# Adding the squares of three norms up to one tile, with the ones product two contraction tiles later

## The reference

```python
def rmsnorm(x, g):
    xf = x.astype(jnp.float32)
    y = xf * lax.rsqrt(jnp.mean(xf * xf, axis=-1, keepdims=True) + EPS)
    return (y * g.astype(jnp.float32)).astype(x.dtype)

def swiglu(x, w_gate, w_up, w_down):
    return (jax.nn.silu(x @ w_gate) * (x @ w_up)) @ w_down

h = h + 0.5 * swiglu(rmsnorm_2(h, ffn1_norm), ffn1_w_gate, ffn1_w_up, ffn1_w_down)
# mixer, the same norm ahead of it; then
h = h + 0.5 * swiglu(rmsnorm_2(h, ffn2_norm), ffn2_w_gate, ffn2_w_up, ffn2_w_down)
```

## Time and profile before

| | |
|---|---|
| median of 3 runs | 1122.43 us (1122.40 to 1123.10) |
| the profiled execution, its own time | 1122.59 us |
| its span in the trace | 1120.8 us |
| granted TensorE clock, mean | 0.998 of full speed |
| TensorE matmuls busy | 1111.9 us (99%), 8968 |
| VectorE, ScalarE, GpSimd busy | 722.6, 664.2, 731.6 us |

### The profile page before, as it was taken

One profiled execution on the slowest core, in us unless ns is written; L12 is line 12 of the kernel. 1 busy time (PEld: TensorE's weight loads), 2 busy tenths in 40 slices (PEclk: granted clock), 3 DMA queues, 4 the chain that ended last, 5 costly groups with the idle time before them and its releaser, 6 DMA issues.

```text
span 1120.8 us, 22358 instructions
## 1 busy us (share of the span) xinstructions
PE 1111.9 (99%) x8968; PEld 1063.0 (95%) x8968; DVE 722.6 (64%) x1275; ACT 664.2 (59%) x1098; POOL 731.6 (65%) x575
## 2 busy tenths in 40 slices
PE   9999999999999999999999999999999999999997
PEld 7888999999988899899999999999899999999997
DVE  5886655577589675375848655556769567655554
ACT  7676754575567577356647544446566547544444
POOL 6787697668488868865865655445865774544442
PEclk9999999999999999999999999999999999999999
DMA  9563354556555534545566766664644655666651
GB/s 335 172 194 119 129 177 150 177 161 216 159 170 188 161 127 151 176 152 170 189 209 207 223 198 193 195 196 144 215 149 134 206 190 169 220 194 190 189 188 38
DMA packets 63895, 199.49 MB, mean 178 GB/s; under 512 B 6992, under 2 KB 17968, under 8 KB 63792
## 3 DMA queue, kind: packets, MB, share of 16 engines
q1 hardware_dynamic: 61920, 194.99, 53.9%
q10 hardware_dynamic: 1872, 3.08, 0.8%
HBM read 196.21 MB, written 1.84 MB: 177 GB/s over the span
## 4 chain that ended last, share of the span: by engine, by line
PE 96%; ACT 2%; DMA 1%; DVE 0%; issue 0%; POOLq 0%; SPq 0%; ACTq 0%
PE ps L1739 51%; PE ps L1837 19%; PE ps L1815 14%; PE ps L1996 2%; PE ps L1788 1%; PE ps L2173 1%; ACT ring L481 1%; PE ps L2093 1%; DMA x<-in_x 1%; PE ps L2070 1%; PE ps L2031 1%; ACT xs L498 0%; PE ps L1970 0%; PE ps L2057 0%; PE ps L2073 0%; PE ps L2094 0%
## 5 line engine op out<-in xcount | busy, mean ns | idle before, releaser
L367 POOL TENSOR_TENSOR ring<-raw,ring 128x512 fp32r<-128x512 f32 x514 | 699.0, 1366 | 364.2 <-ACT ring L481 343.2
L1739 PE MATMUL ps<-xs,ring 128*128 128x256 f32 x5040 | 597.7, 278 | 0.4 <-DVE mq L1049 0.3
L1739 PEld LDWEIGHTS ps<-xs,ring 128*128 128x128 f32 x5040 | 582.9, 188 | 3.6 <-issue 1.3
L481 ACT ACTIVATE ring<-raw 128x1024 fp32r<-128x1024 f32 x364 | 383.2, 1057 | 215.3 <-PE ps L1739 119.3
L1837 PE MATMUL ps<-ys,ring 128*128 128x256 f32 x1920 | 224.4, 276 | 0.0
L1837 PEld LDWEIGHTS ps<-ys,ring 128*128 128x128 f32 x1920 | 220.7, 188 | 0.0
L1011 DVE TENSOR_TENSOR ring<-raw,ring 128x1024 fp32r<-128x1024 f32 x107 | 144.9, 1355 | 69.3 <-ACT ring L481 68.9
L1815 PE MATMUL ps<-ring,xs 128*128 128x512 f32 x672 | 164.9, 397 | 0.0
L1815 PEld LDWEIGHTS ps<-ring,xs 128*128 128x128 f32 x672 | 123.6, 188 | 26.8 <-issue 1.3
L1329 DVE SCALAR_TENSOR_TENSOR ca<-ps,par,ca 128x253 f32<-128x253 f32 (+2 forms) x96 | 46.0, 479 | 34.4 <-ACT ca L564 33.0
L1483 DVE SCALAR_TENSOR_TENSOR ca<-ps,rms 128x256 f32<-128x256 f32 x44 | 18.6, 423 | 48.7 <-PE ps L1739 48.7
(11 more groups left out here) (291 smaller groups left out, 1027.2 us busy)
## 6 DMA issues: line engine op xcount, KB each, us to landing
raw<-in_w SPq DMA_DIRECT2D x364, 512.0 KB, 3.6
y<-bias_rows SPq DMA_DIRECT2D x6, 256.0 KB, 4.3
out_y<-y SPq DMA_DIRECT2D x4, 256.0 KB, 2.4
const<-in_const SPq DMA_DIRECT2D x1, 896.0 KB, 12.3
bias_rows<-lg ACTq DMA_DIRECT2D x1, 768.0 KB, 8.4
x<-in_x ACTq DMA_DIRECT2D x1, 512.0 KB, 4.5
x<-in_x SPq DMA_DIRECT2D x1, 512.0 KB, 6.9
dec<-in_wT ACTq DMA_DIRECT2D x1, 512.0 KB, 3.7
```

The lines of the kernel that those rows point to most:

```text
L367: last = pool.tensor_tensor(ring[:, g % RING, 1, part], raw[:, g % RAW, part], ring[:, g % RING, 0, part].bitcast(F32), ALU.subtract)
L481: act.activation(ring[:, g % RING, 0, :], raw[:, g % RAW, :], ACT.Copy).then_inc(S["hi"], 1)
L1739: last = mm(ps[bank][:, half * T:(half + 1) * T], ring[:, slot % RING, wp, (at + k) * P:(at + k + 1) * P], rhs(k, xp), start=(first and i ...
```

## The change

At the sites n = 2, 3 and 4 (FOLDED is 2) VectorE adds the two halves of the 128x512 tile once more, to 128x256, and signals `sq_sum` after that. TensorE then runs one ones product instead of two, and runs it after six contraction tiles (18 matmuls) of the third slot instead of four. Sites 0 and 1 stay as they are. (FINAL, 5, is the last norm, which has code of its own.)

```diff
@@ -135,6 +135,7 @@
 N_UPDATES = 4
 FINAL = LAYERS + 3
+FOLDED = LAYERS
 FINAL_AT = (LAYERS + 1) * (KT // 2)
@@ -1027,8 +1028,10 @@
                     dve.wait_ge(S["sq"], n * 4 + b + 1)
                     ins = tt(ps[3][:, :] if b < 3 else sqs[:, 0:512], ps[3][:, :], sqs[:, b * 512:(b + 1) * 512],
                              ALU.add)
-                    if b < 3:
+                    if b < 3 or n >= FOLDED:
                         step(ins)
+                if n >= FOLDED:
+                    ins = tt(sqs[:, 0:T], sqs[:, 0:T], sqs[:, T:2 * T], ALU.add)
                 ins.then_inc(S["sq_sum"], 1)
@@ -1722,8 +1725,9 @@
                 pe.wait_ge(S["sq_sum"], n + 1)
-                for c in range(2):
-                    last = mm(ps[4][:, 0:T], ones, sqs[:, c * T:(c + 1) * T], start=(c == 0), stop=(c == 1))
+                parts = 1 if n >= FOLDED else 2
+                for c in range(parts):
+                    last = mm(ps[4][:, 0:T], ones, sqs[:, c * T:(c + 1) * T], start=(c == 0), stop=(c == parts - 1))
                 last.then_inc(S["ssq"], 1)
@@ -1745,9 +1749,10 @@
             def around_squares(bank, slot, n):
 
-                tile_product(bank, 0, slot, xs_part, range(KT // 2), final=False)
+                ahead = 6 if n >= FOLDED else 4
+                tile_product(bank, 0, slot, xs_part, range(ahead), final=False)
                 sum_squares(n)
-                tile_product(bank, 0, slot, xs_part, range(KT // 2, KT), first=False).then_inc(S["slots_used"], 1)
+                tile_product(bank, 0, slot, xs_part, range(ahead, KT), first=False).then_inc(S["slots_used"], 1)
```

## The result

The changed kernel takes **1135.32 us** (median of 4 runs, 1135.15 to 1135.47) against 1122.41 (1122.04 to 1123.10, 4 runs) for the kernel before: 12.9 us slower, a ratio of 1.0115 with an interval of 1.0103 to 1.0127. The profiled execution took 1135.25 us, its span is 1133.5 (before 1120.8). The forecast was 1121.8, range 1120.8 to 1123.3.

A forecast was written before the change was run, and what follows sets the result against it. TensorE, busy 1111.9 of 1120.8 us, was taken as the bound. Gains of 0.34 and 0.32 in the feed-forward parts less 0.06 in the mixer gave 0.60 us: 1121.8 against a median of 1122.43, range 1120.8 to 1123.3.

The forecast's parts named there:

- the one behind the sum: After the three sites' sum of 0.60 us: later stages wait only for this chain's events and shift with it.
- a gain of at most 1.30: TensorE at n = 2, 3, 4: three removed products of 0.433 us, 1.30 us, the whole gain there can be.
- the 0.03 for the unforeseen: Chance of 0.03 given to what the prediction hadn't thought of.
- The product is worth 0.433 us: TensorE, each of three sites: one ones product costs 0.433 us, from four records starting 0.217 us apart.
- The add, 0.4 to 0.65 us and hidden: VectorE, each site: the new 128x256 add takes 0.4 to 0.65 us, hidden from TensorE by six moved matmuls (0.68 us).
- the prediction had 0.25: First feed-forward part: without the six moved matmuls TensorE would wait 0.25 us for the new add.
- The port: VectorE against GpSimd: a two-SBUF-input instruction and a GpSimd SBUF read exclude each other; first issued keeps the port throughout.
- The rival in which the add is caught by a new half: First part and mixer: add waits 1.30 us behind GpSimd, 0.56 late twice, 1123.0; add caught in general, chance 0.10.
- The mean 2.68 us after the tile's first matmul: First feed-forward part: VectorE's mean released 2.68 us after its tile's first matmul, 2.43 before, so 0.25 later.
- The mixer's wait, 0.28 to about 0.8: Mixer, n = 3: TensorE's idle before the fifth tile's load grows from 0.28 to about 0.8 us; loss there 0.06.
- Waits of 0.09 and 0.11 us for the first gate results: Fifth tile's load: TensorE waits 0.09 us in the first feed-forward part, 0.11 in the second; gains 0.34 and 0.32.
- Same, 0.95: Whole kernel: chance 0.95 of a result within 2.24 us of now, which a measurement can't tell from no change.

The follow-up runs named there:

- g1: Kernel before, plus one extra plain float32 product of 256 columns ahead of tile f = 12 of each feed-forward part; 1131.05 us.
- f1: Changed kernel with its single ones product back after four contraction tiles instead of six; 1128.96 us.
- g4: Changed kernel, its single ones product followed by one of 128 columns writing the same values again, still after six tiles; 1129.22 us.
- f2: Kernel before, its two ones products moved from four to six contraction tiles at n = 2, 3, 4, without the added add; 1122.73 us.
- f3: Changed kernel with its single ones product issued twice, the second overwriting the first with the same values; 1123.07 us.
- h1: Changed kernel with the ones product after five contraction tiles and followed by one of 128 columns; 1121.61 us, ratio 0.9993 to the kernel before.
- h2: Same as h1, and in the mixer's scores the two products change places (256 columns first, 128 last); 1122.02 us, ratio 0.9996.
- i1: Changed kernel with the ones product after five contraction tiles, cut into three products of 128 columns (third repeats the first); 1122.72 us.
- g2: Changed kernel, plus two extra plain float32 products of 256 columns ahead of tile f = 12 of each feed-forward part; 1130.19 us.
- f4: Changed kernel with its single ones product cut into two products of 128 columns; 1135.55 us, ratio 1.0116.
- h3: Kernel before, plus one extra plain float32 product of 128 columns ahead of tile f = 12 of each feed-forward part; 1122.94 us.

## Why the prediction was wrong

**The step that failed** is the one behind the sum: "Later stages wait only for events of this same chain and shift with it." It took the distance between TensorE's matmuls, 0.1133 us, for a constant of the stream. It is one of two values that this stream can have, and removing the product switched it: 3132 matmuls that each took 4.45 ns more, 13.9 us, against a gain of at most 1.30. The last sentence of the prediction named a total that moves by more than 1.3 us as what nothing in it explains; no rival had this mechanism, and the 0.03 for the unforeseen was too little. The signs were in the trace of the kernel before: in the mixer tiles of 24 matmuls took 2.83 and 2.74 us in turn, at the same granted clock of 1.00 and with no wait between. Their chain rows, read for spacing and not only for waits, would have given the question what decides between the two. They wouldn't have given the answer.

**Point by point**, for what the edit does at its own place:
- *The product is worth 0.433 us.* Right: two records in 0.43 (chain of g1), four in 0.86. The removal of it was real, and all of it was outweighed.
- *The add, 0.4 to 0.65 us and hidden.* Right: 0.61 at n = 2, with no idle time ahead of the product, and 0.42 at n = 4. In f1, without the moved tiles, TensorE's load came 0.25 us late (12 loads from 596.30 at 0.1133 make 597.66, it came at 597.92; of that the profile shows 0.18 as idle), and the prediction had 0.25.
- *The port.* In the changed kernel a GpSimd half starts at 595.99 and takes 1.30 (before: 596.53 and 1.30), and the add issued at 596.97 ends at 597.58, 0.29 after it. The rule that the prediction weighed (the Trainium skill, SBUF — State Buffer, "Who interferes with whom") agrees: the add was held for the rest of that half, and it came late enough in it to stay covered. The rival in which the add is caught by a new half didn't occur.
- *The mean 2.68 us after the tile's first matmul.* 2.67.
- *The mixer's wait, 0.28 to about 0.8.* It grew to 0.68:

```profile
789.75 10.40 PEld L1743 LDWEIGHTS ps<-xs,ring 128*128 128x128 f32 x91 [0.68 <-DVE mq L1632]
```

- *Waits of 0.09 and 0.11 us for the first gate results.* Not in the changed kernel, where TensorE came later at the wider spacing; in g4, with the 113 spacing kept, they were there at 0.10. Their size was right. Their price wasn't safe: at n = 4 of g4 that wait switched the spacing, and cost over 6 us; in the five other cases of f2, f3 and g4 a wait of this size cost no more than itself.
- *The stretch from the first L1739 to the first L1837 shorter by 0.34* (11.76 to 11.42). It measured 607.77 - 596.12 = 11.65: shorter by 0.11, since 78 matmuls had 4.45 ns more each (0.35) and the forecast wait fell away.
- *Same, 0.95.* The prediction called the same what lies within 2.24 us; the kernel moved by 12.9. That 1.15% would still count as the same by a bound of 2% is no merit of the forecast. With the spacing kept it would have held: f3, h1, h2 and i1 lie within 0.9 us of the kernel before.

**What stays open.** What in TensorE makes two spacings isn't shown. They are 272 and 283 cycles of 2.4 GHz for 256 columns. The Trainium skill (TensorE: Matmul & The Clock Gate, "Back-to-back issue gap") gives a single figure for 256 columns, 262 cycles for one matmul by itself, and says that in a stream of weight loads and matmuls the spacing is set by both together. The page's 262 isn't what was measured here, and the measurement decides; no run here tests its sentence on the two together, since no run changed the loads. Which interruption gives which spacing isn't settled either. Their length orders all the runs with products in plain float32, at 0.22, 0.43, 0.65 and 0.86 us, and the transposes of 0.44 us go against it. From a stream already at 118 it isn't the same table: two products (0.86) bring 113 back (g2, and g1 at the mixer's site), and so did the four short passes of f4 at its mixer's site (0.44), while one product of 0.43 there in the changed kernel and in f1 left 118. And behind a wait of TensorE the outcome went either way: f1's waits, 2 ns apart, gave opposite results. In the mixer it was no different. There a wait of 0.68 us took the changed kernel from 118 to 113 and left g2 at 118, and one of 0.79 us left f2, f3 and f4 at 113 and took g4 to 118. Neither the spacing ahead of a wait nor its length foretells the one behind it.

## What to carry to other kernels

Where TensorE is busy 99% of the time, read the spacing of its matmuls stage by stage (24 in 2.72 or in 2.83), in the kernel before as in the one after; a change of less than a microsecond in what interrupts the stream can move every matmul behind it by 4%. Judge an edit of this kind with its spacing in view, and try it at neighbouring places and lengths before it is dropped: the same idea with half a product more and one tile earlier took 1121.6 us instead of 1135.3, though no gain over the kernel before (1122.5 beside it) is shown. And a wait forecast at 0.1 us can cost more than 0.1 us if it stands inside such a stream: in the feed-forward parts it did so in one case of six, and behind g1's wait of 0.10 us in the mixer too.

## What was unexpected of the hardware

- A stream of weight load and matmul (128x128 weights, 256 columns, rounded operands) has two steady spacings, 113.3 and 117.8 ns, at the same granted clock of 1.00. Each lasts for more than 1500 matmuls when nothing interrupts it.
- Two passes in plain float32, 0.43 us, switch it from the first to the second (g1); four passes, 0.86 us, leave the first alone and switch the second back (f3, g2); two short ones, 0.22 us, leave the first alone (h3).
- Four passes of 128 columns of a plain float32 product, 0.44 us, switch it to the second (f4, n = 2 and 4); four transposes of 128 columns, as long, leave the first alone (before, 117.78 and 407.93).
- A wait of TensorE as short as 0.10 us can switch it (g4, n = 4) or not (g4, n = 2).
